# Attention scores of the first sixteen steps in two PSUM banks per map, with the wait moved back by one step

## The chip, the cores and the metric
The kernel runs on one core of a Trainium2 chip. The metric is device time of one execution in microseconds (us), lower is better; for the kernel before it is the median of three runs. A profile of one further execution is there, with its own time.

## The reference
One layer of a hybrid decoder on a 1024 x 1024 input in float32: RMSNorm, an input projection, three mixers side by side (differential attention, a convolution module, a state-space module), an output projection with residual, and then a top-2-of-32 mixture of experts. The change touches the differential attention alone:

```python
def block(i):                       # 8 tiles of 128 queries
    ...
    def probs(qb, k):
        s = jnp.einsum('bqhd,bkhd->bhqk', qb, k).astype(jnp.float32) * scale + bias
        return jax.nn.softmax(jnp.where(causal, s, -1e30), axis=-1)
    p = probs(q1b, k1) - lam * probs(q2b, k2)
    return jnp.einsum('bhqk,bkhd->bqhd', p.astype(v.dtype), v)
```

So each query tile i and head h has two score maps (m = 0 and m = 1), each a softmax of its own over the keys up to the tile, and their difference is multiplied by v.

## The kernel before, in words
The attention is a software pipeline written out by hand. Step k is query tile i = k // 4 and head h = k % 4, 32 steps in all (NI); nk = 128 (i + 1) keys are live in it, so nk is 128 in steps 0 to 3, 256 in 4 to 7, 384 in 8 to 11 and 512 in 12 to 15. Every engine has one loop `for k in range(ITERS)`, whose body mixes the parts of several steps, and each engine runs its instructions in the order in which they are written:

- TensorE (PE): `scores(k)` (line 1257: the matmuls of both maps), `turn(k-2)` (L1268: transposes of the finished probabilities), `fill(k)` (other matmuls: in steps 0 to 3 those of `unit`, L1114; in steps 4 to 7 none; from step 8 on the output projection, L1303), `times_v(k-3)` (L1277), and in steps 0 and 1 two `misc` groups (L1211).
- VectorE (DVE): `stats(k, 0)` and `stats(k, 1)` (L1670, and L1673, L1674 where nk > 256: scaled scores plus bias, and the row's minimum), then `combine(k-1)` (L1684, L1685, L1687: the two maps into one). In step 3 two large operations of another mixer (L1775, L1776) stand between them.
- ScalarE (ACT): `o_evac(k-4)` (L962, L963), `p_evac(k-2)` (L952), `exps(k, 0)` and `exps(k, 1)` (L941, and L943 where nk > 256).

The waits around the change, by semaphore:
- `scores(k)` waits until e_ok is 2k: both exps of step k-1 have ended. The scores of map m always go to PSUM bank 2m (and from tile 4 on to 2m+1 too, where nk > 512).
- `stats(k)` waits for `scores(k)` (s_ps); `exps(k, m)` waits for `stats(k, m)` (nm_ok).
- `combine(k-1)` waits for `exps(k-1, 1)`; `turn(k-2)` waits for `combine(k-2)` (p_ok); `p_evac(k-2)` waits for `turn(k-2)`.
- `times_v(k-3)` waits for `p_evac(k-3)` and, as there is one bank for its result, for `o_evac(k-4)` (head_ss).

`fill(8)`, the first of the output projection, also waits for the weights w_out, of which the last part (`wout_in[1]`) is issued by the SyncE queue right after the last `unit` matmul, ahead of the first expert's w_up and w_gate.

Of the kernel before, what the change touches and what calls it, by code (L numbers as in the profile page):

```python
# [16 lines left out]
P = 128  # L17
# [5 lines left out]
HEADS, DK, DV = 4, 64, 128  # L23
# [60 lines left out]
def parts_before(k):  # L84
    return sum(parts(j) for j in range(k))

def tile_at(k, off):

    t, r = divmod(k - off, HEADS)  # L90
    return t if r == 0 and 0 <= t < NT else None

def lg_bank(i):
# [15 lines left out]
def build(nc, t):  # L110

    with ExitStack() as ctx:
# [3 lines left out]
        def sem(name):  # L116
            return ctx.enter_context(nc.semaphore(name))
# [27 lines left out]
        qkT = RB[:, :].rearrange("p (c n) -> p c n", c=8)  # L145
# [172 lines left out]
        psum = ctx.enter_context(nc.psum_tensor("psum", [P, 8, 512], F32))  # L318
        def bank(i):
            return psum[:, i, :]  # L320
        def banks(i, n):
            return psum[:, i:i + n, :].rearrange("p b n -> p (b n)")
# [68 lines left out]
        e_ok = sem("e_ok")  # L391
# [243 lines left out]
        def _(pool):  # L635
# [69 lines left out]
            for k in range(ITERS):  # L705
                i = tile_at(k, 7)
                if i is not None:
                    head_scale(i)
                i = tile_at(k, 13)
                if i is not None:  # L710
                    pool.wait_ge(ms2v_ok, i + 1)
                    pool.tensor_tensor(rstd2[:, i:i + 1], ms2v[:, i:i + 1], mhalf[:, 0:1], ALU.pow).then_inc(rstd2_ok, 1)
# [95 lines left out]
        def _(act):  # L808
# [69 lines left out]
            for r in range(4):  # L878
                ins = act.activation(ksb[32 * r:32 * r + GCH, :, P:2 * P],
                                     psum[32 * r:32 * r + GCH, 0, :].rearrange("p (q n) -> p q n", q=4), ACT.Copy)  # L880
# [53 lines left out]
            def exps(k, m):  # L934
                nk = (k // HEADS + 1) * P
                far = max(nk - 256, 0)
                p = p1[k % 3] if m == 0 else p2[k % 2]
                st_ = smx[:, k % 2, m, :]
                nm = st_[:, 2:3] if far else st_[:, 0:1]
                act.wait_ge(nm_ok, 2 * k + m + 1)  # L940
                ins = act.activation(p[:, far:nk], p[:, far:nk], ACT.Exp, bias=nm, scale=-1.0, accum_out=st_[:, 4:5])  # L941
                if far:
                    ins = act.activation(p[:, 0:far], banks(2 * m, 2)[:, 0:far], ACT.Exp,  # L943
                                         bias=nm, scale=SCALE, accum_out=st_[:, 5:6])
                ins.then_inc(e_ok, 1)

# [19 lines left out]
            for k in range(ITERS):  # L966
# [15 lines left out]
                i = tile_at(k, 8)  # L982
                if i is not None:
                    misc(FIRST_HEAD + i)
                i = tile_at(k, 12)
# [100 lines left out]
        def _(pe):  # L1086
# [35 lines left out]
            for i in range(NT):  # L1122
# [3 lines left out]
                for k in range(KD):  # L1126
                    ins = pe.transpose(psum[:, 2 * (i % 2) + k // 4, P * (k % 4):P * (k % 4) + P],
                                       xt[:, i, k * P:(k + 1) * P], ident[:, :])
# [16 lines left out]
            for g in range(GROUPS):  # L1145
                ins = pe.transpose(psum[:, g // 4, P * (g % 4):P * (g % 4) + P],
                                   uc[:, g].rearrange("p i h -> p (i h)"), ident[:, :])
# [3 lines left out]
            for r, vb in enumerate((VBR, VBI)):  # L1151
                for a in range(PAIRS):
                    b = 2 * r + a // 4
                    if a % 4 == 0:
                        pe.wait_ge(uT_ev, b + 1)
                    ins = pe.transpose(psum[:, b, P * (a % 4):P * (a % 4) + P],
                                       vb[:, a].rearrange("p i h -> p (i h)"), ident[:, :])
# [4 lines left out]
            for g in range(GROUPS):  # L1162
# [4 lines left out]
                ins = pe.matmul(out, BBI[q:q + STATES, a, :], CAI[q:q + STATES, a, 0:CHUNK, :].rearrange("p t h -> p (t h)"),  # L1167
                                start=False, stop=True)
# [5 lines left out]
            for r, win_ in enumerate((WinR, WinI)):  # L1174
                for a in range(PAIRS):
                    b = a // 4
                    if r == 1 and a % 4 == 0:
                        pe.wait_ge(vin_ev, b + 1)
                    for q in range(2):
                        ins = pe.matmul(psum[STATES * q:STATES * (q + 1), b, P * (a % 4):P * (a % 4) + P],  # L1180
                                        win_[:, a, STATES * q:STATES * (q + 1)], UT[:, 2 * a + q, :], start=True, stop=True)
# [45 lines left out]
            for a in range(PAIRS):  # L1227
# [6 lines left out]
                for r in range(2):  # L1234
                    ins = pe.matmul(out[r], UT[:, 2 * a + r, :], TG[:, 2 * a + r, :], start=False, stop=True)
# [7 lines left out]
            def scores(k):  # L1243
                i, h = k // HEADS, k % HEADS
                nk = (i + 1) * P
                if k == 0:
                    pe.wait_ge(unit_ev, EARLY_UNITS)
                    pe.wait_ge(y_ev, 4)
                else:
                    pe.wait_ge(e_ok, 2 * k)  # L1250
                if i == 4 and h == 0:
                    pe.wait_ge(unit_ev, len(UNITS))
                for b in range(0, nk, 512):
                    w = min(512, nk - b)
                    for m in range(2):
                        half = slice(DK * m, DK * m + DK)
                        ins = pe.matmul(psum[:, 2 * m + b // 512, 0:w], qkT[half, h, i * P:(i + 1) * P],  # L1257
                                        qkT[half, HEADS + h, b:b + w], start=True, stop=True)
                ins.then_inc(s_ps, 1)

# [74 lines left out]
            for k in range(ITERS):  # L1335
# [15 lines left out]
                i = tile_at(k, 8)  # L1351
                if i is not None:
                    misc(FIRST_HEAD + i)
                for b in range(2):
                    i = tile_at(k, 13 + b)
                    if i is not None and (i < NT - 1 or b):
                        x2_turn(i, b)
                i = tile_at(k, 15)
# [14 lines left out]
            for i in range(NT):  # L1373
                ins = pe.matmul(bank(1)[:, 0:32], onesb[:, :], mbf[:, i, :], start=i == 0, stop=i == NT - 1)
# [3 lines left out]
            for r in range(16):  # L1378
                if r % 8 == 0:
                    pe.wait_ge(tab_ok, r // 8 + 1)  # L1380
                    pe.wait_ge(sl_two, r // 8 + 1)
                ins = pe.matmul(bank(2)[:, 0:2 * NBLK], slot1h[:, r, :], bval[:, r].rearrange("p n v -> p (n v)"),
                                start=r == 0, stop=r == 15)
            ins.then_inc(tab_ps, 1)
            pe.wait_ge(tab_ok, 3)
            for n_ in range(1 + SLOTS):
                ins = pe.matmul(bank(7)[0:1, MAXBLK * n_:MAXBLK * (n_ + 1)], col[0:MAXBLK, n_:n_ + 1], ident[0:MAXBLK, 0:MAXBLK],
                                start=True, stop=True)
# [90 lines left out]
        def _(dve):  # L1479
            n = [0]  # L1480
            def link(ins):
                n[0] += 1
                ins.then_inc(dve_c, 1)
                dve.wait_ge(dve_c, n[0])
# [27 lines left out]
            for v in range(2):  # L1512
                ins = dve.tensor_tensor_reduce(out=ctmp[:, 64 * v:64 * v + DK], in0=lamv[:, 2 * v, :], in1=lamv[:, 2 * v + 1, :],
                                               scale=1.0, scalar=0.0, op0=ALU.mult, op1=ALU.add, accum_out=lam[:, v:v + 1])
# [56 lines left out]
            for base in (1, 2, 4):  # L1571
                w = [P, base, PAIRS]
# [10 lines left out]
            w = [P, PAIRS, GCH]  # L1583
# [3 lines left out]
            for i in range(CHUNK):  # L1587
                dve.tensor_copy(RVR[:, i, :], PWR[:, CHUNK - 1 - i, :])
                ins = dve.tensor_copy(RVI[:, i, :], PWI[:, CHUNK - 1 - i, :])
            link(ins)  # L1590
            w = [P, PAIRS, CHUNK, GCH]
# [17 lines left out]
            for j in range(TAPS - 1, -1, -1):  # L1609
                s = TAPS - 1 - j  # L1610
                for c in range(2):
                    acc = banks(2 - 2 * c, 2)
                    if s == 0:
                        ins = dve.tensor_scalar(acc, convh[:, c, :], convw[:, c, j:j + 1], None, ALU.mult)
                    else:
                        dve.wait_ge(tap_c, 2 * s - 1 + c)
                        ins = dve.scalar_tensor_tensor(acc[:, s:L], convh[:, c, 0:L - s], convw[:, c, j:j + 1],  # L1617
                                                       acc[:, s:L], ALU.mult, ALU.add)
# [3 lines left out]
            for i in range(NT):  # L1622
                ins = dve.bn_stats(lnst[:, i, :], convt[:, i, :])
            link(ins)
            for i in range(NT):
                ins = dve.bn_aggr(lnmv[:, i, :], lnst[:, i, :])
# [14 lines left out]
            for i in range(NT):  # L1641
                ins = dve.tensor_scalar(convt[:, i, :], convt[:, i, :], lnmv[:, i, 0:1], lnr[:, i:i + 1],
                                        ALU.subtract, ALU.mult)
            ins.then_inc(ln_ok, 1)
            y_add(1)
            for i in range(4):
                c, half = i // 2, i % 2
# [8 lines left out]
            def stats(k, m):  # L1656
                i, h = k // HEADS, k % HEADS
                nk = (i + 1) * P
                far = max(nk - 256, 0)
                p = p1[k % 3] if m == 0 else p2[k % 2]  # L1660
                st_ = smx[:, k % 2, m, :]
                S = banks(2 * m, 2)
                if m == 0:
                    dve.wait_ge(s_ps, k + 1)
                    if k >= 2:
                        dve.wait_ge(p_ok, k - 1)
                    if k >= 3:
                        dve.wait_ge(pT_ps, parts_before(k - 2))

                ins = dve.tensor_tensor_reduce(out=p[:, far:nk], in0=S[:, far:nk], in1=band[:, h, 256 - (nk - far):256],  # L1670
                                               scale=-SCALE, scalar=3e38, op0=ALU.add, op1=ALU.min, accum_out=st_[:, 0:1])
                if far:
                    link(dve.tensor_reduce(st_[:, 1:2], S[:, 0:far], AX.X, ALU.max))  # L1673
                    ins = dve.scalar_tensor_tensor(st_[:, 2:3], st_[:, 1:2], -SCALE, st_[:, 0:1], ALU.mult, ALU.min)  # L1674
                ins.then_inc(nm_ok, 1)
# [85 lines left out]
            for k in range(ITERS):  # L1761
                for half in range(2):
                    i = tile_at(k, 10 + 2 * half)
                    if i is not None:
                        x2_half(i, half)
                i = tile_at(k, 13)
# [11 lines left out]
                i = tile_at(k, 7)  # L1778
# [5 lines left out]
                i = tile_at(k, 13)  # L1784
# [4 lines left out]
                for b in range(2):  # L1789
                    i = tile_at(k, 13 + b)  # L1790
                    if i is not None and i < NT - 1:
                        x2_turned(i, b)
                i = tile_at(k, 15)
# [54 lines left out]
            for r in range(2):  # L1848
                ins = dve.tensor_tensor(MP[:, 8 * r:8 * r + 8, :], MM[:, 8 * r:8 * r + 8, :], RK2, ALU.mult)
# [186 lines left out]
```

## Time and profile before

| | |
|---|---|
| median of 3 runs | 1216.95 us (1214.99 to 1218.87) |
| the profiled execution's own time | 1218.94 us |
| its span (first to last instruction) | 1217.2 us |
| TensorE busy | 1141.0 us, 94% |
| VectorE busy | 475.9 us, 39% |
| ScalarE busy | 362.9 us, 30% |
| attention steps 0 to 31 | 289.7 to about 550 us of the span |

### The profile page before, as it was taken

Reading aid. Unit: us, or ns where it says so; the run is one execution under the profiler, and the core shown is the slowest. Engines: PE = TensorE matmul, PEld = TensorE weight load, DVE = VectorE, ACT = ScalarE, POOL = GpSimd, SP = SyncE. Lnnn points to the kernel's source line nnn. Section 1 sums busy time; section 2 is a strip of 40 time slices with the busy share of each in tenths; the row PEclk is TensorE's granted clock in tenths of the full one; section 3 lists DMA queues with packets and bytes.
Section 4 is the critical chain, followed back from the end, with each engine's and each line's share of the span. In section 5 each row is a group of like instructions: output and inputs, shape, how many; then the busy total and the mean of one; then the engine's idle time right before and its main releaser. Section 6 shows DMA issues by size and latency. Waiting matters only on the chain.

```text
span 1217.2 us, 16326 instructions
## 1 busy us (share of the span) xinstructions
PE 1141.0 (94%) x5082; PEld 548.6 (45%) x5083; DVE 475.9 (39%) x1033; ACT 362.9 (30%) x732; POOL 291.1 (24%) x226
## 2 busy tenths in 40 slices
PE   6999999998899999996899999988999999999981
PEld 5897444454455666655333333322333333333320
DVE  3550029952456665446232322312232322323234
ACT  3121100025455555412223323222323223223222
POOL 0110199930000000101112122122212222122233
PEclk9999999999899999997899999989999999999995
DMA  8127111022411111177682999999799999999344
GB/s 257 26 36 145 35 35 35 0 69 75 173 43 62 53 53 51 55 306 296 252 341 38 382 374 376 410 414 413 282 365 379 392 406 377 401 383 389 130 140 181
DMA packets 86270, 262.59 MB, mean 216 GB/s; under 512 B 31973, under 2 KB 49132, under 8 KB 61630
## 3 DMA queue, kind: packets, MB, share of 16 engines
q1 hardware_dynamic: 68868, 243.43, 52.1%
q0 software_dynamic: 11632, 17.44, 6.2%
q10 hardware_dynamic: 5706, 0.92, 0.4%
q8 instruction: 34, 0.56, 0.2%
q14 instruction: 30, 0.25, 0.1%
HBM read 245.38 MB, written 27.00 MB: 224 GB/s over the span
## 4 chain that ended last, share of the span: by engine, by line
PE 86%; DMA 6%; ACT 2%; DVE 2%; issue 1%; POOL 1%; SPq 1%; ACTq 0%; DVEq 0%; POOLq 0%
PE psum L1411 27%; PE psum L1430 13%; PE psum L1114 13%; PE psum L1303 9%; PE psum L1111 4%; PE psum L1257 3%; DMA W<-in_w_gate 3%; PE psum L1397 3%; PE psum L1277 3%; PE psum L1109 3%; PE psum L1268 2%; PE psum L1418 2%; DMA W<-x_rows 1%; PE psum L1332 1%; DMA W<-in_x 1%
## 5 line engine op out<-in xcount | busy, mean ns | idle before, releaser
L1411 PE MATMUL psum<-W,RD 128*64 (+1 forms) x800 | 372.1, 609 | 15.0 <-DVE RD L1933 14.1
L1412 PE MATMUL psum<-W,RD 128*64 128x512 f32 x800 | 372.1, 609 | 0.0
L1411 PEld LDWEIGHTS psum<-W,RD 128*64 128x64 f32 x800 | 107.4, 140 | 228.6 <-issue 222.7
L1915 DVE TENSOR_TENSOR RD<-psum,RD 128x256 f32<-128x256 f32 x50 | 21.2, 425 | 420.5 <-ACT RD L1028 420.5
L1430 PE MATMUL psum<-W,RD 128*64 (+1 forms) x400 | 184.6, 605 | 0.7 <-ACT RD L1032 0.7
L1431 PE MATMUL psum<-RD 128*64 128x512 f32 x400 | 184.6, 605 | 0.0
L727 POOL DMA_INDIRECT x_rows<-RD,tabi x48 | 77.8, 1621 | 443.4 <-ACT RD L1039 433.7
L1114 PE MATMUL psum<-W 128*128 128x512 f32 x384 | 166.4, 593 | 0.6 <-ACT W L845 0.6
L1303 PE MATMUL psum<-W,RD 128*128 128x512 f32 x256 | 118.8, 597 | 1.6 <-ACT RD L921 1.1
L1114 PEld LDWEIGHTS psum<-W 128*128 128x128 f32 x384 | 72.5, 190 | 89.7 <-issue 88.7
L1412 PEld LDWEIGHTS psum<-W,RD 128*64 128x64 f32 x800 | 107.4, 140 | 0.0
L1024 ACT ACTIVATE RD<-W 128x2048 f32 (+1 forms) x50 | 95.2, 1903 | 23.7 <-DMA W<-in_w_down 23.7
L1430 PEld LDWEIGHTS psum<-W,RD 128*64 128x64 f32 x400 | 51.2, 138 | 94.2 <-issue 88.3
L1039 ACT ACTIVATE RD<-psum,xr 128x512 f32<-128x512 f32 x49 | 33.7, 689 | 194.8 <-PE psum L1431 194.8
L1617 DVE SCALAR_TENSOR_TENSOR psum<-W,pv,psum 128x1023 f32<-128x1023 f32 (+29 forms) x60 | 70.6, 1283 | 0.0
L720 POOL DMA_INDIRECT RD<-h_rows,tabi x54 | 57.3, 1061 | 46.7 <-DVE tabi L1888 21.0
L1931 DVE COPY W<-W 128x2048 f32 x49 | 60.4, 1233 | 16.2 <-DMA W<-in_w_gate 14.5
L1028 ACT ACTIVATE RD<-psum 128x256 f32<-128x256 f32 x50 | 19.2, 385 | 153.1 <-PE psum L1412 153.0
L1303 PEld LDWEIGHTS psum<-W,RD 128*128 128x128 f32 x256 | 45.2, 192 | 41.6 <-issue 39.3
L1936 DVE COPY W<-W 128x2048 f32 x49 | 59.7, 1219 | 0.0
L1111 PE MATMUL psum<-W 128*128 128x256 f32 x256 | 56.9, 380 | 0.0
L1431 PEld LDWEIGHTS psum<-RD 128*64 128x64 f32 x400 | 51.2, 138 | 0.0
(340 smaller groups left out, 1275.3 us busy)
## 6 DMA issues: line engine op xcount, KB each, us to landing
W<-in_w_up SPq DMA_DIRECT2D x32, 2048.0 KB, 12.9
W<-in_w_gate SPq DMA_DIRECT2D x32, 2048.0 KB, 18.2
W<-in_w_down SPq DMA_DIRECT2D x32, 2048.0 KB, 20.3
W<-in_x SPq DMA_DIRECT2D x16, 512.0 KB, 4.5
W<-in_w_in SPq DMA_DIRECT2D x5, 1024.0 KB, 12.0
W<-in_w_in SPq DMA_DIRECT2D x16, 256.0 KB, 4.3
x_rows<-W SPq DMA_DIRECT2D x8, 512.0 KB, 2.9
h_rows<-RD SPq DMA_DIRECT2D x8, 512.0 KB, 3.5
```

The lines of the kernel that those rows point to most:

```text
L727: pool.indirect_dma_start(x2_half, bass.IndirectOffsetOnAxis(ap=rows, axis=0), y, None, bounds_check=2 * L - 1, oob_is_err=False, compute_ ...
L1024: act.activation(down1, src[:, :, 1, :], ACT.Copy).then_inc(ex_cd, 1)
L1111: ins = pe.matmul(out[:, 0:WCH], hT[:, k, i * P:(i + 1) * P], w[:, k, :], start=first, stop=last)
L1114: ins = pe.matmul(out, w[:, k, ct * P:(ct + 1) * P], hT[:, k, 512 * half:512 * half + 512], start=first, stop=last)
L1303: ins = pe.matmul(bank(proj_bank(j)), mixT[:, c, i * P:(i + 1) * P], wout[:, c, 512 * half:512 * half + 512], start=c == 4, stop=c == 3)
L1411: pe.matmul(bank(2)[0:HALF].rearrange("p (g n) -> p g n", g=2), x, near, start=k == 0, stop=k == KD - 1)
L1412: ins = pe.matmul(bank(2)[HALF:P], x, upgate1[:, k].rearrange("p g n -> p (g n)"), start=k == 0, stop=k == KD - 1)
L1430: pe.matmul(out[0:HALF], a, W[:, bass.ds(base + (2 * KD * FF + D * k), 512)], start=k == 0, stop=k == FK - 1)
L1431: ins = pe.matmul(out[HALF:P], a, down1[:, k, :], start=k == 0, stop=k == FK - 1)
L1617: ins = dve.scalar_tensor_tensor(acc[:, s:L], convh[:, c, 0:L - s], convw[:, c, j:j + 1], acc[:, s:L], ALU.mult, ALU.add)
L1931: dve.tensor_copy(dst[:, :, 0:4], src[:, :, 0:4]).then_inc(ex_cu, 1)
L1936: dve.tensor_copy(dst[:, :, 4:8], src[:, :, 4:8]).then_inc(ex_cu, 1)
```

## The change
For the first four tiles (k < 16), where a map's scores fit into one bank, the scores of step k go to bank 2m + k % 2 instead of bank 2m, and `scores(k)` waits for the exps of step k-2 (e_ok at 2k-2) instead of step k-1. The readers of the scores, `stats` on VectorE and the second exp on ScalarE, address the same bank. From step 16 on everything is as before, step 16 itself with the full wait. No instruction is added or taken away.

```diff
+def two_banks(k):
+    return k < 4 * HEADS
...
                 if far:
-                    ins = act.activation(p[:, 0:far], banks(2 * m, 2)[:, 0:far], ACT.Exp,
+                    ins = act.activation(p[:, 0:far], (bank(2 * m + k % 2) if two_banks(k) else banks(2 * m, 2))[:, 0:far], ACT.Exp,
                                          bias=nm, scale=SCALE, accum_out=st_[:, 5:6])
...
                 if k == 0:
                     pe.wait_ge(unit_ev, EARLY_UNITS)
                     pe.wait_ge(y_ev, 4)
-                else:
+                elif not two_banks(k):
                     pe.wait_ge(e_ok, 2 * k)
+                elif k >= 2:
+                    pe.wait_ge(e_ok, 2 * k - 2)
...
-                        ins = pe.matmul(psum[:, 2 * m + b // 512, 0:w], qkT[half, h, i * P:(i + 1) * P],
+                        ins = pe.matmul(psum[:, 2 * m + (k % 2 if two_banks(k) else b // 512), 0:w], qkT[half, h, i * P:(i + 1) * P],
                                         qkT[half, HEADS + h, b:b + w], start=True, stop=True)
...
-                S = banks(2 * m, 2)
+                S = bank(2 * m + k % 2) if two_banks(k) else banks(2 * m, 2)
```

## Rows read from the trace of the kernel before

**Rows 1.** The page: TensorE's busy time, and the chain that ended last by engine.

```profile
PE 1141.0 (94%) x5082; PEld 548.6 (45%) x5083; DVE 475.9 (39%) x1033; ACT 362.9 (30%) x732; POOL 291.1 (24%) x226
...
PE 86%; DMA 6%; ACT 2%; DVE 2%; issue 1%; POOL 1%; SPq 1%; ACTq 0%; DVEq 0%; POOLq 0%
```

**Rows 2.** Who PE waited for, 314 to 345 us (total, times, longest).

```profile
PE psum L1257 <- ACT W L941: 3.9, 4, 1.2
PE psum L1268 <- DVE xr L1687: 0.4, 1, 0.4
```

**Rows 3.** Stages by window: length, busy of PE, PEld, DVE, ACT, POOL, PEclk, DMA, GB/s.

```profile
283.60:287.20 3.60, 2.02 (x13) 1.26 (x12) 0.00 (x0) 3.60 (x5) 0.00 (x0) 1.00 0.00 0
316.40:319.20 2.80, 1.39 (x9) 0.73 (x7) 2.41 (x11) 2.45 (x10) 0.00 (x0) 1.00 0.65 165
319.20:321.60 2.40, 1.19 (x9) 0.67 (x9) 1.55 (x7) 1.95 (x9) 0.00 (x0) 0.95 1.04 428
321.60:324.90 3.30, 2.27 (x10) 1.34 (x10) 1.57 (x8) 1.97 (x9) 0.00 (x0) 0.50 1.02 432
328.20:335.30 7.10, 7.10 (x22) 3.59 (x22) 2.29 (x11) 2.59 (x12) 1.05 (x1) 0.76 0.33 135
335.30:549.00 213.70, 211.95 (x1029) 128.28 (x1028) 119.39 (x392) 105.56 (x330) 20.16 (x22) 1.00 0.25 91
549.00:620.00 71.00, 58.09 (x291) 29.67 (x292) 28.25 (x95) 16.71 (x19) 11.65 (x11) 0.83 0.76 294
```

**Rows 4.** Timeline of PE: start, length, line, and the idle time before it.

```profile
316.46 0.70 PE L1257 MATMUL psum<-W 64*128 64x256 f32 x4
317.54 0.33 PE L1268 MATMUL psum<-ident,xr 128*128 128x128 f32 x1 [0.37 <-DVE xr L1687]
...
319.23 0.70 PE L1257 MATMUL psum<-W 64*128 64x256 f32 x4 [1.07 <-ACT W L941]
319.86 0.33 PE L1268 MATMUL psum<-ident,W 128*128 128x128 f32 x1
320.02 0.39 PE L1277 MATMUL psum<-W 128*128 128x128 f32 x2
321.59 1.22 PE L1257 MATMUL psum<-W 64*128 64x256 f32 x4 [1.18 <-ACT W L941]
...
324.89 1.23 PE L1257 MATMUL psum<-W 64*128 64x256 f32 x4 [1.02 <-ACT W L941]
...
328.18 1.65 PE L1257 MATMUL psum<-W 64*128 64x384 f32 x4 [0.60 <-ACT W L941]
...
330.24 4.28 PE L1303 MATMUL psum<-W,RD 128*128 128x512 f32 x8
...
335.33 0.92 PE L1257 MATMUL psum<-W 64*128 64x384 f32 x4
336.18 0.44 PE L1268 MATMUL psum<-ident,W 128*128 128x128 f32 x2
336.45 3.60 PE L1303 MATMUL psum<-W,RD 128*128 128x512 f32 x8
```

**Rows 5.** Timeline of ACT and DVE in step 5, in order of time.

```profile
319.08 0.35 ACT L962 ACTIVATE RD<-psum,rl 128x128 f32<-128x128 f32 x1
...
319.58 0.20 ACT L963 ACTIVATION_READ_ACCUMULATOR psum<-psum,rl 128x1 f32 x1
...
319.98 0.42 DVE L1670 CUSTOM_DVE_ANT_0 xr<-psum,band 128x256 f32<-128x256 f32 x1 [0.86 <-PE psum L1257]
...
320.22 0.28 ACT L952 ACTIVATE W<-psum 128x128 f32<-128x128 f32 x1 [0.45 <-PE psum L1268]
...
320.44 0.51 ACT L941 ACTIVATE xr<-xr,smx 128x256 f32<-128x256 f32 x1
...
320.67 0.16 DVE L1684 RECIPROCAL rl<-smx 128x2 f32<-128x2 f32 x1
...
321.12 0.48 DVE L1687 SCALAR_TENSOR_TENSOR W<-W,smx 128x256 f32<-128x256 f32 x1
...
321.44 0.35 ACT L962 ACTIVATE RD<-psum,rl 128x128 f32<-128x128 f32 x1
```

**Rows 6.** DMA issues, 316 to 316.6 us: count, size, time to landing.

```profile
W<-in_w_out SPq DMA_DIRECT2D x1, 1024.0 KB, 4.9
```

## Prediction
> **What bounds the kernel now.** I read the page first: TensorE is busy 94% of the span and 86% of the chain that ended last [rows 1]. So a wait that is taken away pays only where TensorE itself stands still, and the next view to read is who TensorE waited for in the steps that the change touches. Around steps 5 to 8 it lists four waits of `scores` (L1257) for the exps (L941), 3.9 us together, and one of `turn` for `combine` [rows 2]. The timeline puts the four at steps 5, 6, 7 and 8: 1.07, 1.18, 1.02 and 0.60 us [rows 4]. The reader should see why only there: steps 4 to 7 have no fill, so after `times_v(k-3)` TensorE has nothing until the exps of the same step are through. Steps 0 to 3 have the `unit` and `misc` matmuls between two scores, and no wait of L1257 for an exp stands in the list for them (the first of the four is step 5). From step 8 on the fill is there, and from 335.3 to 549 us TensorE is busy 211.95 of 213.70 us [rows 3]. Of the sixteen steps that the diff names, then, four can gain.
>
> The windows by stage show a second cost in the same place: the granted clock is 1.00 in step 4, 0.95 in step 5, 0.50 in step 6, and comes back only in step 8 (0.76 over its window) [rows 3]. So it fell from 2.4 to 1.2 GHz after two steps in which TensorE was busy 1.39 of 2.80 and 1.19 of 2.40 us. The same instructions show its price: scores of 256 keys take 0.70 us at 2.4 GHz and 1.22 at 1.2; scores of 384 keys 1.65 against 0.92; the fill of eight records 4.28, of which the last part ran at full clock, against 3.60 [rows 4].
>
> **The change, part by part.** Nothing is added or removed in work; the bank in the address costs nothing on any engine (the same element counts). What moves is the start of `scores(k)`, from behind `exps(k-1, 1)` to behind `exps(k-2, 1)`, which in steps 5 to 8 has long ended. I follow what is late next.
>
> Behind `scores(k)` in TensorE's order stand `turn(k-2)`, which needs `combine(k-2)`, and `times_v(k-3)`, which needs `o_evac(k-4)`. The latter comes behind `exps(k-1, 1)` in ScalarE's order. So the wait isn't gone, it moves: TensorE may now do `scores(k)` and `turn(k-2)` while ScalarE does the exps of k-1, and stops at `times_v(k-3)` instead. The loop then runs at ScalarE's pace, if that is the slowest. ScalarE's step with 256 keys: `o_evac` 0.60 (319.08 until 0.10 before the accumulator read of 319.58 ends, as two ACT records overlap by that much), `p_evac` 0.28 (0.39 with two chunks, overlapped to about 0.3), both exps 1.00 (320.44 to 321.44) [rows 5]: 1.9 us. VectorE's: stats from 319.98 to 320.67 and combine from 320.67 to 321.60 with two chunks: 1.62 us [rows 5]. TensorE's at full clock: scores 0.63 (319.23 to 319.86), turn 0.27 (336.18 to 336.45), `times_v` 0.3 to 0.5: 1.2 to 1.4 us [rows 4]. So 1.9 us per step, against 2.36 (319.23 to 321.59) at full clock and 3.30 (321.59 to 324.89) at half.
>
> Now step by step, with about 0.05 us for each hand-off, as between 319.93 and 319.98 [rows 4, 5]. `scores(4)`, `turn(2)` (held by VectorE's large operation until 317.54, unchanged) and `times_v(1)` stay. `scores(5)` starts at 318.0 instead of 319.23. Its stats run from 319.1 (VectorE is in `combine(3)` until then) to 319.8, `combine(4)` to 320.7. On ScalarE `o_evac(1)` ends at 319.8 as before; `p_evac(3)` and the exps of step 5 follow at once and end at 320.95, then `o_evac(2)` to 321.55, `p_evac(4)`, exps of step 6 to 322.85, `o_evac(3)` to 323.45, exps of step 7 to 324.7. TensorE: `times_v(2)` at 319.85, `scores(6)` 320.1, `turn(4)` 320.8, `times_v(3)` 321.6, `scores(7)` 321.9, `turn(5)` 322.55, `times_v(4)` 323.5 (0.45), `scores(8)` 323.95 (0.85, from 335.33 to 336.18 [rows 4]), `turn(6)` 324.8 and `fill(8)` at 325.1 instead of 330.24: 5.15 us earlier. The fill then runs at full clock from its start, 3.60 instead of 4.28 [rows 4]: 0.68 more. The sum is 5.8 us. My hand-offs are the shortest that the rows show and every one of four steps has several, so I give back 0.2 us a step and take 5.0.
>
> `fill(8)` has one other condition near it: the last part of w_out, issued at 316.3 and landed 4.9 us later [rows 6], so at about 321.3. Cover: 3.8 us before the new start. From step 8 on nothing changes on TensorE, and the earlier end of the attention moves the router, whose inputs all follow from it, and then the experts by as much. So I pass the 5.0 us through whole.
>
> The sum is against the profiled execution's own 1218.94 us (1217.2 of span and 1.7 around it), which lies 2.0 us above the median. I put it on the median, 1216.95, because the other executions run the same instructions: 1216.95 - 5.0 = 1212.0 us. A difference of 0.3%, 3.65 us, is about what a measurement of this kernel can tell from none.
>
> **The clock is the part least certain.** Of the 5.8 us some 2.4 come from the loop alone: with 2.4 GHz all through, the old loop would have gone 319.23, 321.59, 323.95 and 326.4 for `scores(5)` to `scores(8)`, with `fill(8)` at 327.5, against 325.1. The other 3.4 are that the clock doesn't fall. What speaks for it: in the new steps TensorE is busy 1.2 to 1.4 of 1.9 us, some 65 to 70%, against half in the two steps ahead of the fall [rows 3]. And in a stretch with 2.02 of 3.60 us busy, 56%, the clock stayed at 1.00 [rows 3]. So what TensorE will do lies above a share that kept the clock.
>
> The Trainium skill (TensorE: Matmul & The Clock Gate, "A second HAM failure mode: psum-queue depth-cycling") says that a kernel that cycles through PSUM banks in each iteration leaves small idle times between groups of matmuls, often enough for the clock to go back and forth. That speaks against this change, which begins to alternate banks; by that rule the result would be the first rival's below, by the rows it is the forecast.
>
> **Rivals.**
> 1. *The clock falls all the same.* The small gaps at `times_v` remain, 0.3 to 0.9 us a step. If it falls where it did (late in step 5), then from `scores(7)` on work takes TensorE about 1.2 us for scores, 0.5 for turn and 0.9 for `times_v`, 2.6 a step instead of ScalarE's 1.9, and `scores(8)` 1.6: `scores(7)` 322.15, `turn(5)` 323.3, `times_v(4)` 323.8, `scores(8)` 324.8, `fill(8)` 326.8, and 0.7 of the fill's gain is lost as well. Gain 3.4 us: 1213.5.
> 2. *The new wait takes the old one's place, and there is little clock to win.* If the fall is not in most executions of the kernel before (the trace is of a slow one, 1218.94), the median can win only the loop's part, 2.4 us less 0.8 for hand-offs: 1.6 to 2.4, so about 1214.9. For it: the range of the three runs, 3.9 us, is of the size of the clock's part. Against it: the half-idle stretch of steps 4 and 5 is in the program itself.
> 3. *Weights.* If w_out lands late because w_up and w_gate run with it at 432 GB/s [rows 3], `fill(8)` can't move. The DMA share is still 0.33 in the window of step 8, from 328.2 to 335.3 [rows 3], so the last of the three ended soon after 328.2, and the gain would be nil at worst: 1217. The landing time of 4.9 us [rows 6] speaks against it.
> 4. *Slower.* The earlier end puts the router and the first experts elsewhere against the clock. There, from 549 to 620 us, the mean granted clock is 0.83 [rows 3], so 0.34 of 71 us ran at 1.2 GHz, 24 us, and a fully busy TensorE loses half of that. If a shift of 5 us adds low time, it decides from 10 us of it on (5 us lost); with 20 us more the time would be 1222. Nothing in the trace leads there rather than the other way.
>
> **How the numbers follow.** Forecast 50%, rival 1 24%, rival 2 15%, rival 3 3%, rival 4 5%, and 3% that nothing moves for a reason I don't see. The likeliest has its own range from 1210.0 (the sum whole and another microsecond of clock time won later) to 1213.5. The range for 8 in 10 takes in rivals 1 and most of 2 above, and below a little more clock time won in the router: 1208.5 to 1216.0. Faster by over 0.3% (under 1213.3): nearly all of the forecast, 0.45, half of rival 1, 0.12, and a little of 2 by the medians' own spread: 0.59. Slower 0.05. The rest, 0.36, is within 0.3%.
>
> **What would show it in the profile after.** The four waits of L1257 for L941 are gone from steps 5 to 8, and in their place TensorE waits at L1277 for L963 (`o_evac`), some 1.5 us in all. `scores(5)` starts 1.2 us earlier against `scores(4)`; from `scores(4)` to `fill(8)` it is 8.6 us instead of 13.8; PEclk reads 1.00 in steps 5 to 8, and the fill takes 3.60. The step from `scores(6)` to `scores(7)` is 1.8 to 2.1 us. Wrong would be: a clock of 0.50 again (rival 1), `fill(8)` waiting for a DMA (rival 3), or the attention ending 5 us earlier with the span unchanged (rival 4).

## The result, and the profile after

The changed kernel takes 1209.51 us (median of 12 runs, 1208.45 to 1213.33); the kernel before took 1215.58 us in the 12 runs that go with it. The ratio is 0.9947, 95% interval 0.9936 to 0.9957: 0.53% faster, some 6.1 to 6.4 us, with an interval from 5.2 to 7.8 us.

The page of the changed kernel, span and busy times:

```profile
span 1208.0 us, 16326 instructions
...
PE 1133.5 (94%) x5082; PEld 545.2 (45%) x5083; DVE 475.3 (39%) x1033; ACT 362.3 (30%) x732; POOL 292.0 (24%) x226
```

The number of instructions is the same; TensorE's busy time is 7.5 us shorter [rows 1], though nothing was taken from it, and that is already a sign of the clock. Who TensorE waited for from 314 to 345 us (total, times, longest), to be read beside [rows 2]:

```profile
PE psum L1283 <- ACT psum L967: 1.1, 3, 0.4
PE psum L1274 <- DVE W L1693: 0.4, 1, 0.4
PE psum L1274 <- DVE xr L1693: 0.4, 1, 0.4
```

The four waits of `scores` for the exps, 3.9 us, are gone. In their place stand three of `times_v` (now L1283) for `o_evac` (L967), 1.1 us together, and `turn(3)` waits 0.37 us for `combine(3)`, which VectorE starts late because of its large operations in step 3. (The other wait of `turn`, `turn(2)` for `combine(2)`, stood in the kernel before too.) The timeline of TensorE, beside [rows 4]:

```profile
316.38 0.70 PE L1263 MATMUL psum<-W 64*128 64x256 f32 x4
317.45 0.33 PE L1274 MATMUL psum<-ident,xr 128*128 128x128 f32 x1 [0.37 <-DVE xr L1693]
317.62 0.46 PE L1283 MATMUL psum<-W 128*128 128x128 f32 x2
318.01 0.70 PE L1263 MATMUL psum<-W 64*128 64x256 f32 x4
319.08 0.33 PE L1274 MATMUL psum<-ident,W 128*128 128x128 f32 x1 [0.37 <-DVE W L1693]
319.83 0.46 PE L1283 MATMUL psum<-W 128*128 128x128 f32 x2 [0.42 <-ACT psum L967]
320.22 0.70 PE L1263 MATMUL psum<-W 64*128 64x256 f32 x4
...
321.58 0.46 PE L1283 MATMUL psum<-W 128*128 128x128 f32 x2 [0.29 <-ACT psum L967]
321.97 0.70 PE L1263 MATMUL psum<-W 64*128 64x256 f32 x4
...
323.44 0.68 PE L1283 MATMUL psum<-W 128*128 128x128 f32 x4 [0.34 <-ACT psum L967]
324.05 0.92 PE L1263 MATMUL psum<-W 64*128 64x384 f32 x4
...
325.17 3.60 PE L1309 MATMUL psum<-W,RD 128*128 128x512 f32 x8
```

From `scores(4)` to `fill(8)` it is 8.79 us (316.38 to 325.17); before it was 13.78 [rows 4]. The fill lasts 3.60 instead of 4.28. Together 5.67 us. The stages by window (length, busy of PE, PEld, DVE, ACT, POOL, PEclk, DMA, GB/s), beside [rows 3]:

```profile
318.00:320.20 2.20, 1.41 (x8) 0.74 (x7) 1.96 (x11) 2.20 (x11) 0.00 (x0) 1.00 0.93 361
320.20:321.97 1.77, 1.48 (x10) 0.80 (x9) 1.51 (x8) 1.77 (x9) 0.00 (x0) 1.00 1.05 440
321.97:324.05 2.08, 1.74 (x12) 1.02 (x11) 1.84 (x10) 2.08 (x11) 0.38 (x1) 1.00 1.01 429
```

ScalarE is busy for the whole of each step, and `times_v` waits for it in each: it sets the pace now. The granted clock stays at 1.00, so TensorE never leaves 2.4 GHz here.

The two profiled executions lie further apart than the medians: 9.2 us. Of these, 5.67 us are the steps above; the other 3.5 us come behind `fill(8)`. Windows over the same piece of work, the router's last part and the first expert block, in the kernel before and then in the changed one:

```profile
573.00:585.00 12.00, 10.90 (x37) 3.92 (x38) 0.69 (x1) 0.06 (x1) 2.94 (x3) 0.72 0.26 77
```

```profile
567.00:576.00 9.00, 7.94 (x37) 3.38 (x38) 0.69 (x1) 0.03 (x1) 2.89 (x3) 1.00 0.36 102
```

The same 37 records take 10.90 us at a mean clock of 0.72 and 7.94 at 1.00. From the end of `fill(8)` to the end of the span the kernel before has 882.8 us, the changed one 879.4, and all the profiles of the experiments below lie between 877.2 and 880.4, whatever wait they have. banks_only below, which has the waits of the kernel before, has 879.4. So the 3.5 us belong to that one execution of the kernel before, not to the change.

### The profile page after: what moved, and what is told of

The parts are those of the page before. It is cut to its first block, busy times and chain, and to the rows that moved or that the text cites. A ratio compares the mean times of both kernels' runs of the same rounds, so it can differ in the third digit from the quotient of the medians.

```text
span 1208.0 us, 16326 instructions
## 1 busy us (share of the span) xinstructions
PE 1133.5 (94%) x5082; PEld 545.2 (45%) x5083; DVE 475.3 (39%) x1033; ACT 362.3 (30%) x732; POOL 292.0 (24%) x226
## 4 chain that ended last, share of the span: by engine, by line
PE 86%; DMA 6%; ACT 2%; DVE 2%; issue 1%; POOL 1%; SPq 1%; ACTq 0%; DVEq 0%; POOLq 0%
PE psum L1417 27%; PE psum L1436 13%; PE psum L1118 13%; PE psum L1309 9%; PE psum L1115 4%; DMA W<-in_w_gate 3%; PE psum L1263 3%; PE psum L1283 3%; PE psum L1403 3%; PE psum L1113 3%; PE psum L1424 2%; PE psum L1274 2%; PE psum L1338 1%; DMA W<-x_rows 1%; DMA W<-in_x 1%
## 5 line engine op out<-in xcount | busy, mean ns | idle before, releaser
L1032 ACT ACTIVATE RD<-psum 128x256 f32<-128x256 f32 x50 | 19.2, 384 | 154.0 <-PE psum L1418 154.0
```

## The experiments

The question was what the gain is made of: the loop (scores started earlier), the clock (no stretch at 1.2 GHz), or something that the banks do by themselves; and whether the new wait at `times_v` is worth a further edit. Since all times end up in one stage, I read each profile by one length as well: from the first `unit` record of step 2 to the end of `fill(8)` (taken as the start of the matmul behind it, since the records overlap by 0.16 us or so), for brevity "the stage". It holds the same work in every kernel, but for seven added transposes a step in one.

| kernel | ratio to before (95%) | stage, us | scores(4) to fill(8), us | clock in steps 5 to 8 |
|---|---|---|---|---|
| before | 1 | 25.87 | 13.78 | falls in step 5 |
| banks_only | 1.0001 (0.9989 to 1.0013) | 26.88 | 13.77 | falls in step 5 |
| steps_5_6 | 0.9976 (0.9957 to 0.9994) | 23.62 | 11.72 | falls late in step 6 |
| steps_7_8 | 0.9962 (0.9947 to 0.9976) | 23.50 | 12.10 | falls in step 5 |
| steps_6_8 | 0.9962 (0.9951 to 0.9973) | 22.49 | 10.87 | falls in step 7 |
| before_busy | 0.9965 (0.9950 to 0.9980) | 22.70 | 11.29 | 1.00 |
| after | 0.9947 (0.9936 to 0.9957) | 20.19 | 8.79 | 1.00 |
| after_again | 0.9957 (0.9939 to 0.9975) | 20.20 | 8.79 | 1.00 |
| steps_5_8 | 0.9959 (0.9941 to 0.9977) | 20.20 | 8.79 | 1.00 |
| o_banks | 0.9944 (0.9923 to 0.9965) | 19.75 | 8.33 | 1.00 |
| spread | 0.9930 (0.9913 to 0.9948) | 19.24 | 9.54 | 1.00 |
| spread_again | 0.9933 (0.9915 to 0.9951) | 19.22 | 9.54 | 1.00 |
| spread_o | 0.9944 (0.9932 to 0.9956) | 19.29 | 9.53 | 1.00 |
| spread_w | 0.9929 (0.9914 to 0.9944) | 19.08 | 9.33 | 1.00 |

The stage of one profile is sharp to some 0.05 us where the clock holds (three times 20.2, twice 19.2); the intervals of the whole times are some 3 to 5 us wide. So the ratios decide the large questions and the stage the small ones.

**banks_only: the banks without the moved wait.**

```diff
-                elif not two_banks(k):
+                elif not two_banks(k) or not (False):
                     pe.wait_ge(e_ok, 2 * k)
```

The new condition is always true, so every step has the full wait again.

> The alternating banks alone: every step waits for the exps of the step before, as in the kernel before. Theory (the moved wait is the gain): no change, within 2 us of the kernel before; TensorE again waits about 3.9 us at the scores of steps 5 to 8, and the clock is 0.50 in steps 6 and 7. Rival (the banks themselves matter, by less contention between TensorE's writes and the readers): some 2 us faster, with shorter stats or exps. Rival (the bank cycling makes the clock go back and forth): slower by 2 us or more, with more low stretches.

Its wait of `scores` for the exps, 314 to 345 us, and then two windows:

```profile
PE psum L1263 <- ACT W L945: 3.6, 4, 1.1
```

```profile
318.00:319.80 1.80, 0.81 (x6) 0.48 (x7) 0.87 (x6) 1.54 (x7) 0.00 (x0) 0.99 0.95 389
319.80:330.00 10.20, 7.66 (x27) 4.40 (x27) 5.05 (x25) 5.79 (x24) 2.07 (x2) 0.50 1.01 426
```

No change: 1.0001. The waits are back and so is the one long stretch at 0.50. The banks do nothing by themselves, neither for nor against; what they are for is that the wait can move. Alternating them did not make the clock go back and forth. The trace does not agree with what the prediction took from the Trainium skill (TensorE: Matmul & The Clock Gate, "A second HAM failure mode: psum-queue depth-cycling"), that cycling through banks brings small idle times and a clock that goes back and forth: here what idles TensorE is the wait, not the bank. The page's kernel has bf16 matmuls of N = 512, and no run here is of that kind. The low stretch lasted longer here than in the kernel before (its fill took 5.30 us, not 4.28) with nearly the same waits (3.6 and 3.9 us). So the stage of a kernel whose clock falls is sharp to about 1 us only.

**steps_5_6 and steps_7_8: the early wait in two of the four steps only.**

```diff
-                elif not two_banks(k):
+                elif not two_banks(k) or not (5 <= k <= 6):
```

This is steps_5_6; in steps_7_8 the condition is `7 <= k <= 8`.

> The early wait only in steps 5 and 6, the full one elsewhere. Theory (a loop part and a clock part, the clock decided by how idle steps 4 and 5 are): the scores of step 6 start at about 320.2, those of 7 at 322.7 and those of 8 at 325.0; the clock stays at 1.00, and the fill of step 8 starts at about 326.1, 4.1 us earlier than before, and is 0.7 shorter: 4.8 us faster. Rival (gain by the waits' lengths alone, 1.07 and 1.18 us): 2.3 us faster.

> The early wait only in steps 7 and 8. Theory (the clock has fallen by then): the clock is 0.50 in steps 6 to 8 as before, the fill of step 8 starts at about 328.5, 1.7 us earlier, and a part of that is lost as it runs longer at half clock: 1 to 1.5 us faster. Rival (all steps alike): half of the whole gain, 2.9 us.

Windows of steps_5_6:

```profile
320.00:322.00 2.00, 1.72 (x10) 1.05 (x10) 1.73 (x10) 2.00 (x10) 0.00 (x0) 1.00 1.06 442
322.00:324.00 2.00, 1.29 (x6) 0.52 (x5) 0.70 (x2) 1.46 (x7) 0.00 (x0) 0.61 0.99 422
324.00:326.00 2.00, 1.60 (x8) 1.25 (x6) 1.63 (x8) 1.21 (x5) 0.88 (x1) 0.50 1.04 430
```

My expectation for steps_5_6 missed: the clock did fall, only later, at about 322.5, and the scores of step 7, right behind it, took 1.22 us. The early starts themselves were as expected (3.85 and 6.37 us behind `scores(4)` for steps 6 and 7; expected 3.7 and 6.2). So 2.25 us of the stage were won instead of the 4.8 expected. The rival of steps_5_6 (the waits' lengths alone, 2.3 us) can't be told from this result; but it would give the whole change 3.9 us, and that has 5.67.

Two rows of steps_7_8, `scores(8)` and `fill(8)`:

```profile
327.08 1.65 PE L1263 MATMUL psum<-W 64*128 64x384 f32 x4
...
328.94 3.60 PE L1309 MATMUL psum<-W,RD 128*128 128x512 f32 x8
```

Here the clock was 0.50 from step 6 on, and the fill started 12.1 us behind `scores(4)`, both as expected. But 2.4 us of the stage were won, more than my 1 to 1.5: the clock came back at 328.6, before the fill, which ran at full clock (3.60). That is nearer to this run's rival (half of the whole gain, 2.9 us) than to its theory, and so is the whole time (0.24 to 0.53% faster, 2.9 to 6.4 us). Each half keeps a stretch at 1.2 GHz, which the whole does not have; as its length differs between executions, I don't divide these two results further.

**before_busy: no moved wait, but work of no use inside the waits.**

```diff
                 if 3 <= k < NI + 3:
                     times_v(k - 3)
+                if 4 <= k < 8:
+                    for _ in range(7):
+                        pe.transpose(bank(1)[:, 0:P], ident[:, :], ident[:, :])
```

> The kernel before, with seven transposes of the identity into the unused PSUM bank 1 behind times_v in steps 4 to 7, some 0.8 us of work with no use inside each wait of about 1.1 us. Theory (3.4 of the 5.8 us are the clock): the clock stays at 1.00, the scores of steps 5 to 8 start at 319.2, 321.6, 324.0 and 326.4, the fill at 327.5 at full clock: 3.4 us faster than the kernel before, though TensorE has more to do. Rival (the gain is the earlier scores, the clock is a passenger): no gain, or up to 0.5 us slower.

Its timeline of TensorE and one window of it:

```profile
318.15 0.93 PE L1350 MATMUL psum<-ident 128*128 128x128 f32 x7
319.38 0.70 PE L1257 MATMUL psum<-W 64*128 64x256 f32 x4 [0.30 <-ACT W L941]
...
321.75 0.70 PE L1257 MATMUL psum<-W 64*128 64x256 f32 x4 [0.41 <-ACT W L941]
...
324.27 0.70 PE L1257 MATMUL psum<-W 64*128 64x256 f32 x4 [0.46 <-ACT W L941]
...
326.79 0.92 PE L1257 MATMUL psum<-W 64*128 64x384 f32 x4 [0.24 <-ACT W L941]
...
327.91 3.60 PE L1303 MATMUL psum<-W,RD 128*128 128x512 f32 x8
```

```profile
322.00:324.00 2.00, 1.81 (x15) 1.24 (x13) 1.43 (x7) 1.44 (x6) 0.00 (x0) 1.00 1.00 426
```

28 transposes more, and the kernel is 0.35% faster (2.4 to 6.1 us), the stage 3.17 us shorter. The order, the banks and the semaphores are those of the kernel before. `scores(5)` and `scores(6)` start 2.76 and 5.13 us behind `scores(4)`, as before (2.77 and 5.13), and TensorE still waits 0.24 to 0.46 us for the exps at each `scores`, so the transposes neither hasten nor delay one; what differs is the clock. So the clock is worth 3.2 of the 5.67 us (4.2 if banks_only is taken as the kernel before), and the loop the other 2.5 (22.70 against 20.2, both at full clock). It also shows that the fall is the usual case in the kernel before and not that of one unlucky profile: otherwise its median would not move.

**after_again and steps_5_8: is it the same each time, and is it these four steps?**

```diff
-                elif not two_banks(k):
+                elif not two_banks(k) or not (5 <= k <= 8):
```

This is steps_5_8; after_again has no edit.

> The changed kernel once more, beside the three below. Theory (in its steps TensorE is busy enough, so the clock holds in every execution): a second profile shows 8.8 us from the scores of step 4 to the fill of step 8 and a granted clock of 1.00 up to the end of the attention; 6 us faster than the kernel before. Rival (the clock held by luck in the one profile): a stretch at 0.50 in steps 6 to 8 and a gain of 3 to 4 us.

> The early wait only in steps 5 to 8, the full one in all the other steps. Theory (the gain comes from these four steps alone): equal to the changed kernel within 1 us, with no wait for the exps at the scores of any other step. Rival (the freedom in steps 9 to 15 matters too): 1 to 3 us slower than the changed kernel, with waits at the scores of steps 9 to 15.

Both as the theory said, counting the profile of the result: three profiles with 8.79 us and a clock of 1.00, and no time between the changed kernel and one that has the early wait in steps 5 to 8 alone (0.9957 and 0.9959 on the same chip). The other twelve steps of the diff do nothing.

**steps_6_8: one of the four waits put back.**

```diff
-                elif not two_banks(k):
+                elif not two_banks(k) or not (6 <= k <= 8):
```

> The changed kernel with the full wait put back in step 5 alone. Theory (each wait counts by what it moves, and the clock by how busy TensorE is in steps 4 to 6): the loop loses 0.65 us; whether the clock holds is what this run is for: if it does, the fill of step 8 starts 9.4 us behind the scores of step 4 and the kernel is 0.6 us slower than the changed one. Rival (one wait of 1.1 us is enough for the clock to fall): a stretch at 0.50, and 2 to 4 us slower than the changed kernel.

Windows:

```profile
319.20:321.00 1.80, 1.51 (x11) 0.96 (x11) 0.94 (x6) 1.35 (x7) 0.00 (x0) 1.00 1.06 437
321.00:323.00 2.00, 1.20 (x10) 0.57 (x6) 1.76 (x11) 2.00 (x9) 0.00 (x0) 1.00 0.97 412
323.00:325.00 2.00, 1.56 (x10) 0.96 (x10) 1.76 (x10) 2.00 (x10) 0.30 (x1) 0.91 1.05 446
325.00:327.00 2.00, 2.00 (x7) 0.81 (x6) 0.46 (x1) 1.33 (x7) 1.77 (x2) 0.50 0.98 406
```

The rival in this run's expectation holds in the profile: the clock fell near the end of the window 323 to 325, and the stage is 2.3 us longer than the changed kernel's, of which I had put 0.65 down to the loop. The whole time says it less sharply: 0.9962 against 0.9947 and 0.9957. One wait of 1.06 us more can be enough to lose the clock. Whether it falls in every execution of this kernel I can't say from one profile: it took 1212.31 us, and eight of the eleven runs were faster (median 1210.72), so it may hold in some.

**o_banks: the wait that replaced the old one.** The results of `times_v` of steps 1 and 3 go to bank 5, which is free then, so `times_v` need not wait for the last `o_evac`.

```diff
+def o_bank(k):
+    return 5 if k in (1, 3) else 6
...
-                if k:
-                    pe.wait_ge(head_ss, k)
+                if k == 1:
+                    pe.wait_ge(misc_ev, 16)
+                elif k:
+                    pe.wait_ge(head_ss, k - 1 if k <= 4 else k)
```

> The changed kernel with the results of times_v of steps 1 and 3 in bank 5, so that times_v no longer waits for the evacuation of the step before in this stage. Theory (ScalarE paces the steps, 1.85 us each): the 1.1 us of waits at times_v go, the fill of step 8 starts at most 0.3 us earlier, the same time as the changed kernel. Rival (that wait has become the limit): 1.1 us faster than the changed kernel.

```profile
PE psum L1278 <- DVE W L1699: 1.0, 2, 0.6
PE psum L1278 <- DVE xr L1699: 0.8, 2, 0.5
```

These are all of TensorE's waits from 314 to 345 us; L1278 is `turn` here. The waits at `times_v`, 1.1 us, are gone, and those of `turn` for `combine` grew from 0.8 to 1.8 us. 0.45 us of the stage is won, a little over the 0.3 of the theory and well under the 1.1 of the rival. So ScalarE and VectorE pace the steps, and TensorE only waits for them in another place.

**spread, spread_again, spread_o, spread_w: work of use inside the waits.** If TensorE idles in steps 4 and 5 and is full in steps 2 and 3, the last `unit` can be divided differently.

```diff
-                if k in (1, 3):
-                    evac(EARLY_UNITS + k // 2)
+                if k in (1, 5):
+                    evac(EARLY_UNITS + k // 5)
...
-                if k < 4:
-                    unit(EARLY_UNITS + k // 2, 4 * (k % 2) + 2 * part, 2)
+                if k < 2:
+                    unit(EARLY_UNITS, 4 * k + 2 * part, 2)
+                elif k < 6:
+                    at, n = {(2, 1): (0, 2), (3, 0): (2, 2), (3, 1): (4, 2), (4, 1): (6, 1), (5, 1): (7, 1)}.get((k, part), (0, 0))
+                    if n:
+                        unit(EARLY_UNITS + 1, at, n)
```

> The changed kernel with the last unit's eight parts spread over steps 2 to 5 as 2, 4, 1, 1 instead of 4, 4 in steps 2 and 3, so that some of TensorE's work falls into the waits of steps 4 and 5. Theory (TensorE still stands 1.9 us in steps 4 to 7 while ScalarE paces): the scores of step 3 start 1.7 us earlier, and of this 1 us is left at the fill of step 8: 1 us faster than the changed kernel. Rival (the weights of the projection, issued behind the last unit, come later): the fill of step 8 waits for a DMA, and nothing is won or 1 us lost.

> The two versions that beat the changed kernel in one: the last unit's parts over steps 2 to 5, and the second bank for the results of times_v. Theory (each takes away another of TensorE's waits): no wait at times_v, the fill of step 8 0.3 to 0.5 us earlier than in spread, so 0 to 0.5 us faster than it, about 8 us faster than the kernel before. Rival (ScalarE paces anyway): the same time as spread.

> spread_o, with the first expert's w_up and w_gate issued only when the last part of w_out has landed. Theory (in spread_o the fill of step 8 waited for w_out, whose 5.2 us from issue to landing are long because w_up and w_gate run beside it): w_out lands in 3 to 3.5 us, the fill starts as soon as turn(6) is through, 0.4 to 0.5 us earlier against the fill of step 2, and the stage from there to the end of the fill of step 8 takes 18.8 us. Rival (w_out lands no earlier, the time is latency): 19.3 us as in spread_o. In the whole time neither can be told from spread.

> spread once more, on the same chip as spread_w. Theory: 19.2 us from the fill of step 2 to the end of the fill of step 8, against 20.2 in the changed kernel; 0.5 to 0.6% faster than the kernel before. Rival (the 0.70% of the first measurement is real, something else is won later): 0.7% again, with less time behind the fill of step 8 than the changed kernel's 879.3 to 880.4 us.

spread has a stage of 19.24 us, 0.96 less than the changed kernel's 20.2, as expected, and 0.70% in the first measurement. Its six runs (1206.64 to 1208.60) all lie under the seven of the changed kernel on the same chip (1208.82 to 1213.82). Repeated, it was 0.67%. So it beats both kernels. The distance to the changed kernel is 0.96 us in the stage and 2.75 in the medians, and for the difference I have no cause: the time behind the stage was 877.6 and 878.7 us in its two profiles, in the lower half of what all kernels show. Its issue of w_out, and its fill:

```profile
318.77 0.38 SPq L583 DMA_DIRECT2D W<-in_w_out  x1
```

```profile
324.05 3.60 PE L1313 MATMUL psum<-W,RD 128*128 128x512 f32 x8
```

w_out now stands behind the last `unit` matmul in step 5, and landed 5.0 us after its issue, at 323.8. So the room in front of the fill, 3.9 us in the changed kernel, is down to 0.3 us here, and the rival in this run's expectation was only just missed.

spread_o brought the second bank but no more time, and the profile shows why: TensorE's fill starts at 324.60, and w_out, issued at 319.34, takes 5.2 us to land, 324.54. The fill in the timeline, and the DMA view of spread_o from 318 to 320.2 us:

```profile
324.60 3.67 PE L1319 MATMUL psum<-W,RD 128*128 128x512 f32 x8 [0.32 <-issue]
```

```profile
W<-in_w_out SPq DMA_DIRECT2D x1, 1024.0 KB, 5.2
```

The view names no releaser for the 0.32 us; that it is the transfer is inferred from its landing 0.06 us before the fill, here and again in the next run. So the transfer is here the bound that was only a rival in the prediction. In spread_w, w_up and w_gate wait until w_out is there:

```diff
             sp.dma_start(wout[:, 4:6], wo[:, 4:6]).then_inc(wout_in[1], 16)
+            sp.wait_ge(wout_in[1], 16)
             load_up(0)
```

Its SyncE queue in order of time, and then the DMA view:

```profile
319.07 0.38 SPq L587 DMA_DIRECT2D W<-in_w_out  x1
324.05 0.38 SPq L569 DMA_DIRECT2D W<-in_w_up  x1
```

```profile
W<-in_w_out SPq DMA_DIRECT2D x1, 1024.0 KB, 5.0
```

My theory of 3 to 3.5 us fell: with no other weights under way the transfer still took 5.0 us, so sharing with the two others cost it 0.2 at most. The fill started at 324.13, 0.08 us behind the issue of w_up, which waits for the same landing. `turn(6)` had started at 323.56, so without w_out the fill could have started some 0.3 us earlier: the transfer is still the bound.

## Why the prediction was right

The forecast was 1212.0 us and faster; measured were 1209.5 and 0.53%. By its own steps:

- *TensorE bounds, and only steps 5 to 8 can gain*: right. steps_5_8 equals the changed kernel.
- *The banks cost nothing*: right, banks_only.
- *The wait moves to `times_v`, and ScalarE paces*: right. The three waits are 1.1 us against the "some 1.5 us" forecast; the step from `scores(6)` to `scores(7)` is 1.75 us, just under the 1.8 to 2.1 named. The 0.37 us at `turn(3)` for `combine(3)` was not among the waits I listed.
- *The sum*: 5.15 us to the fill and 0.68 in it were worked out; 4.99 and 0.68 came. 8.79 us from `scores(4)` to `fill(8)` stand against 8.6.
- *The term that was mis-sized*: the 0.8 us given back "0.2 us a step" for longer hand-offs. They cost 0.16 us in all (5.15 less 4.99). Without that deduction the forecast would have been 1211.1.
- *3.4 us for the clock, 2.4 for the loop*: measured 3.2 and 2.5, by before_busy. The loop's part is between two kernels at full clock; the clock's part depends on how long the low stretch of the kernel before lasts, and is 3.2 to 4.2.
- *Passed through whole*: the spans behind the stage agree within 3.2 us in all profiles but that of the kernel before, with no trend by the wait, so nothing speaks against it; it can't be shown more sharply than that.
- The base: I put the sum on the median of three runs, 1216.95; over the 12 runs it was 1215.58. 1.4 of the 2.5 us between forecast and result are that, and 0.7 are the stage's 5.67 against 5.0; the last 0.4, between the stage and the medians (6.1), is within the noise.

The rivals: the first, that the clock falls all the same, did not come in the changed kernel, but steps_5_6 and steps_6_8 show how near it is. The second, little clock to win, is excluded by before_busy, whose median would not have moved. The third, the weights, had 3.9 us of room (w_out issued at 316.26, landed 5.0 us later, fill at 325.17) and became true in spread_o. The fourth, lost time in the router and the experts, is in no profile.

The step that was right with a weak reason, and so in part by luck, is the clock's: I had argued that it holds because TensorE's busy share, 65 to 70% of a step, lies above that of a stretch that kept it, 56%. The share came out as forecast or higher (1.41 of 2.20, 1.48 of 1.77 and 1.74 of 2.08 us in the windows above, 64 to 84%). But in steps_6_8 the clock fell after windows of 1.51 of 1.80 and 1.20 of 2.00 us and within one of 1.56 of 2.00, more than 56% in each. So the comparison with that stretch could not tell which way it would go; what decides it stays open.

## What to carry to other kernels

A wait of TensorE can cost more than its length where it comes several times in a row with little work between: here 3.9 us of waits removed, of which 1.5 came back elsewhere (1.1 at `times_v`, 0.4 at `turn`), gave 5.7, since more than half of the gain was that a stretch at 1.2 GHz did not occur. Before rebuilding a pipeline for that, fill the waits with work, at best work that has to be done anyway (the spread unit, 1 us more), or even transposes of no use, and see what the clock alone gives. And when a wait is taken away, write down the next one of each engine and the transfer behind it: ScalarE's and VectorE's steps and then the weights' landing were the limits that came next, and in spread_o the landing ate the 0.3 us that the second bank for `times_v` would have added to spread.

## What the runs showed of the hardware that I had not expected

- 28 transposes of no use, 3.7 us of TensorE's time by their records, made the kernel 0.35% faster (0.20 to 0.50%), by keeping the granted clock at 1.00.
- With one wait of 1.06 us for the exps put back, ended at 319.49, the clock fell at about 324.6 (steps_6_8), out of a stretch in which TensorE was busier (1.20 of 2.00 us in its idlest window) than in one that kept 2.4 GHz, 2.02 of 3.60 [rows 3].
- A transfer of 1 MB took 5.0 us from issue to landing with no other weights under way (spread_w), and 4.9, 5.0 and 5.2 with 4 MB issued right behind it (the kernel before [rows 6], after, spread_o): what stood behind it in the queue cost it 0.2 us at most.
